# Projections with split sources: the products of a half piece in three passes, the last two half pieces by token tiles, and the norms' ends in another order

## The reference

```python
    # block 1
    merged = jax.nn.sigmoid(ga) * (ret @ w_ret_o[l]) + jax.nn.sigmoid(gb) * (att @ w_att_o[l])
    x = x + gt_a[:, None, :] * (merged @ w_o[l])
    h = modulate(rms_norm(x, g_ffn[l]), sh_f, sc_f)
...
    # block 3
    x = x + g1 * (y @ w_out[l])
    h = _rmsnorm(x, norm_ffn[l]) * (1.0 + sc2) + sh2
    u = _causal_dwconv(h @ w_up[l], conv_w[l], conv_b[l])
    u_gate, u_val = jnp.split(u, 2, axis=-1)
    x = x + g2 * ((jax.nn.silu(u_gate) * u_val) @ w_down[l])
    return _rmsnorm(x, norm_final)
```

## Time and profile before

| | us |
|---|---|
| median of 3 runs | 3537.41 |
| lowest, highest | 3537.24, 3542.29 |
| the profiled execution | 3540.02 |
| its span | 3538.3 |
| TensorE busy | 3362.9 (95% of the span), 19988 matmuls |
| DVE, ACT, POOL busy | 2047.3, 1769.5, 1046.0 |
| mean granted clock of TensorE | 0.978 |

### The profile page before, as it was taken

How to read it: one execution, slowest core, us unless ns; L and a number is a source line. 1 busy time by engine, 2 the same in 40 slices (tenths; PEclk the granted TensorE clock), 3 DMA queues, 4 the chain that set the end, 5 groups by cost and what they waited for, 6 DMA issues and landing times. The chain is left out here.

```text
span 3538.3 us, 53413 instructions
## 1 busy us (share of the span) xinstructions
PE 3362.9 (95%) x19988; PEld 2685.3 (76%) x19988; DVE 2047.3 (58%) x2355; ACT 1769.5 (50%) x2330; POOL 1046.0 (30%) x432
## 2 busy tenths in 40 slices
PE   7999999989999999999999898999999997799997
PEld 4778777768888888888888673778887766678876
DVE  3320121279999999999999725511153165346665
ACT  3322333258887878788888634432243342233333
POOL 1334222313223232323222140144443410034443
PEclk9999999989999999999999999999999988999999
DMA  8223443359999999999999737223222310022221
GB/s 278 96 72 101 125 125 125 116 205 383 378 381 370 385 367 389 367 385 375 375 378 378 264 111 264 73 94 95 96 89 79 98 40 4 7 72 95 96 95 42
DMA packets 247405, 696.18 MB, mean 197 GB/s; under 512 B 20030, under 2 KB 151858, under 8 KB 188644
## 3 DMA queue, kind: packets, MB, share of 16 engines
q1 hardware_dynamic: 237364, 658.52, 50.0%
q0 software_dynamic: 9792, 35.66, 3.8%
q10 hardware_dynamic: 112, 0.03, 0.0%
HBM read 668.90 MB, written 29.71 MB: 197 GB/s over the span
## 5 line engine op out<-in xcount | busy, mean ns | idle before, releaser
L350 POOL TENSOR_TENSOR split_w<-ring,split_w 128x1024 fp32r<-128x1024 f32 (+1 forms) x294 | 703.1, 2392 | 1569.4 <-ACT split_w L345 1492.5
L2284 DVE TENSOR_TENSOR moe_low<-ring,moe_high 128x2048 fp32r<-128x2048 f32 x408 | 929.2, 2284 | 56.8 <-ACT moe_high L2274 51.8
L2274 ACT ACTIVATE moe_high<-ring 128x1024 fp32r<-128x1024 f32 x810 | 833.4, 1063 | 123.5 <-PE psum L2525 121.4
L345 ACT ACTIVATE split_w<-ring 128x1024 fp32r<-128x1024 f32 (+1 forms) x294 | 304.3, 1036 | 970.5 <-PE psum L550 593.8
L2521 PE MATMUL psum<-moe_high,moe_xe 128*128 128x512 f32 x2176 | 585.3, 391 | 0.0
L2521 PEld LDWEIGHTS psum<-moe_high,moe_xe 128*128 128x128 f32 x2176 | 409.5, 188 | 82.4
L2433 POOL DMA_INDIRECT moe_y_rows<-moe_ye,moe_target x33 | 193.4, 5862 | 663.4 <-DVE moe_ye L2340 663.4
L550 PE MATMUL psum<-pair,split_w 128*128 128x512 f32 x1488 | 338.2, 389 | 0.0
L2525 PE MATMUL psum<-moe_low,moe_xe 128*128 128x512 f32 x1088 | 336.6, 391 | 0.1
L550 PEld LDWEIGHTS psum<-pair,split_w 128*128 128x128 f32 x1488 | 279.1, 188 | 59.7 <-issue 1.7
L550 PE MATMUL psum<-b_pair,split_w 128*128 128x512 f32 x1344 | 309.5, 391 | 0.0
(11 more groups left out here) (641 smaller groups left out, 4233.9 us busy)
## 6 DMA issues: line engine op xcount, KB each, us to landing
ring<-in_w_experts SPq DMA_DIRECT2D x408, 1024.0 KB, 8.6
ring<-in_w_mod SPq DMA_DIRECT2D x48, 1024.0 KB, 6.5
ring<-in_w_in SPq DMA_DIRECT2D x72, 512.0 KB, 5.1
ring<-in_w_up SPq DMA_DIRECT2D x33, 1024.0 KB, 5.1
ring<-in_w_in SPq DMA_DIRECT2D x25, 1024.0 KB, 5.5
ring<-in_w_down SPq DMA_DIRECT2D x20, 1024.0 KB, 5.1
ring<-in_w_gate SPq DMA_DIRECT2D x11, 1024.0 KB, 5.3
ring<-in_w_out SPq DMA_DIRECT2D x8, 1024.0 KB, 5.3
```

What stands on the lines that cost most here:

```text
L345: self.nc.scalar.activation(high, raw, ACT.Copy).then_inc(self.K.rounded, 1)
L350: self.nc.gpsimd.tensor_tensor(low, raw, high.bitcast(F32), ALU.subtract).then_inc(self.K.split, 1)
L2274: self.nc.scalar.activation(self.B["high"][:, j % HALVES, :], self.raw(j), ACT.Copy).then_inc(self.high, 1)
L2284: self.nc.vector.tensor_tensor(flat(self.low_of(j, 2)), self.K.ring[:, self.ring_slot(j // 2), :], high, ALU.subtract).then_inc(self.low, 2)
```

## The change

Six things change. (1) A half piece of kind N is multiplied in three passes over the tiles: high by high, which waits for the two rounded parts alone; low source by high weights, which waits for `a_split`; high by low weights, which waits for `split`. The last half piece of unit 0 stays in one pass where tiles are counted. (2) The last two half pieces of unit 1 are done together by `last_pieces`, tiles 0 to 2 of the one, then of the other, then tile 3 of both, so that tile 0 is complete after 24 of the last 48 matmuls, tile 1 after 30, tile 2 after 36, tile 3 after 48. (3) `DOWN_ROWS` puts the chunk of two rows second in each unit of a down projection instead of last. (4) `high_ahead` stands behind the norm's ACT steps. ACT scales tile 0 alone, and its order is square 0, root 0, square 1, root 1, square 2, scale 0, square 3, roots 2 and 3. (5) The final norm's DVE steps stand between the additions of the tiles. (6) In b2_rest the square root comes after both halves of the last chunk are rounded.

```diff
+DOWN_ROWS = ((0, 4), (4, 2), *((k, 4) for k in range(6, FFN_T, 4)))
...
-            if j == units and i == 0 and eng is nc.scalar:
+            if j == units and i == 0 and eng is nc.scalar and not tiles:
                 W.high_ahead(nc.scalar)
...
                     after.act_tiles(eng)
+                    W.high_ahead(eng)
...
+        def last_pieces(pe, out):
+
+            at = units * per - 2
+            for piece, t in ((0, 0), (0, 1), (0, 2), (1, 0), (1, 1), (1, 2), (0, 3), (1, 3)):
+                i = at + piece
+                n, place = order[i]
+                r, nr = rows_of[n, place]
+                w = W.ready(pe, n, place)
+                pe.wait_ge(a_split, min(i, per - 1) + 1 if held else i + 1)
+                x = part_of(i)[:, :, 0:nr, :]
+                for k in range(nr):
+                    for a, b in ((0, 0), (1, 0), (0, 1)):
+                        ins = nc.tensor.matmul(out[:, t, :], x[:, a, k, t * P:(t + 1) * P], w[:, b, k, :], start=False,
+                                               stop=(r + k == total - 1 and b == 1))
+                if t == NT - 1:
+                    W.used(ins, place)
+                elif piece:
+                    ins.then_inc(tiles, 1)
...
+                    by_tile = tiles and i == (j + 1) * per - 1
+                    for parts_now in ([((0, 0), (1, 0), (0, 1))] if by_tile else [((0, 0),), ((1, 0),), ((0, 1),)]):
+                        w = W.ready_high(pe, n, place)
+                        if not paired:
+                            pe.wait_ge(a_high, source_no)
+                        if (0, 1) in parts_now:
+                            W.ready(pe, n, place)
+                        if (1, 0) in parts_now and not paired:
+                            pe.wait_ge(a_split, source_no)
+                        for t in range(NT):
+                            for k in range(nr):
+                                for a, b in parts_now:
...
-        self.scaled_by_act = (0, 1) if gated else ()
+        self.scaled_by_act = (0,) if gated else ()
...
-        square(0)
-        for t in range(NT):
-            if t < NT - 1:
-                square(t + 1)
+        for t in range(2):
+            square(t)
             root(t)
-            if t in (1, 2):
-                scale(t - 1)
+        square(2)
+        scale(0)
+        square(3)
+        for t in (2, 3):
+            root(t)
...
+    def dve_tile(self, ve, t):
+
+        if t:
+            self.dve_var(ve, t - 1)
+        if t > 1:
+            ve.wait_ge(self.loaded, 16)
+            self.dve_out(ve, t - 2)
+        if t == NT - 1:
+            self.dve_var(ve, t)
+            self.dve_out(ve, 2)
+            self.dve_out(ve, 3)
...
                     if j == 2:
                         evacuate(0)
+                    if j == 3:
                         sc.wait_ge(var, 1)
```

53 lines of the change are left out of this document (24 added, 29 removed).

## The result

| | before | after |
|---|---|---|
| median, us | 3537.41 (3536.60 to 3547.16, 5 runs) | 3518.59 (3511.24 to 3521.33, 5 runs) |
| the profiled execution | 3540.02 | 3516.78 |
| its span | 3538.3 | 3514.9 |
| TensorE busy | 3362.9 | 3357.8 |
| mean granted clock | 0.978 | 0.982 |

The ratio of the runs is 0.9935, 95% interval 0.9924 to 0.9946: 23 us faster (19 to 27). The two medians alone differ by 18.8. The forecast was 3524.4, 13.0 faster. The sign was right, the size was not.

What follows compares the result with a forecast made beforehand. TensorE is busy 95% of the span, so gains lie where it stands still or work follows its last matmul. Terms 2.2 + 1.0 + 2.1 + 3.9 + 3.8 = 13.0 from the median 3537.4 gave 3524.4, range 3518 to 3531.

Steps and rivals of the forecast that it cites:

- (1) b2_rest: In b2_rest, with the root behind both roundings, TensorE's wait of 2.21 us goes: gain 2.2, between 0 and 2.2.
- (2) b2_down: In b2_down's products, 2.8 us lost before and 1.8 to 1.9 after: gain 1.0, between 2.0 and -0.5.
- (3) b3_down: In b3_down's products, 9.1 us lost before and 6.9 after: gain 2.1, between 5 and -1.5.
- the 1.6 that I put down to 1.2 GHz: At the unit's end in b3_down before: 1.6 us counted as lost because TensorE ran at 1.2 GHz from 3460.3 to 3463.6.
- (4) the end: At the program's end, last tile written 7.1 us after the last matmul instead of 11.0: gain 3.9 (3.0 to 4.5).
- (5) the tails: Norms behind w_o, b3_out, b2_down and b2_out: gains of 0.7, 1.2, 1.5 and 0.4 us, together 3.8.
- I take 7.4: Behind w_o and b3_out, first evacuation 7.4 us after the last matmul, at 1.2 GHz, instead of 5.6 at 2.4 GHz.
- more clock freed: Rival: two or three stretches at 1.2 GHz in the tails vanish, giving 3519.5; chance 0.11 (3516 to 3521).
- (6): high_ahead behind the norm's last root on ACT costs nothing while ACT's wait covers it; the pass boundaries also cost 0.
- The boundaries: 134 added pass boundaries in 67 half pieces cost 0; the rival had 0.188 us each, 3549.6, chance 0.04 (above 3540).
- the first rival: POOL's split starts before DVE's last scaling in three norms, 1.2 us a stage: 3528; chance 0.13, shared with stops kept.

Runs made afterwards that it cites:

- s3_ends_alone: The kernel before with only the norm's order, the final norm's DVE steps and the root of b2_rest changed; 3537.76 us, ratio 0.9982 to before.
- s4_no_rows: The changed kernel with the chunk of two rows last in each unit again; 3523.42 us, ratio 0.9945 to before.
- s8_before_fill: The kernel before with transposes of the identity in TensorE's gaps in the tails behind w_o and b3_out; one trace, 3536.99 us.
- s2_passes_alone: The kernel before with half pieces in three passes and their waits, everything else as before; 3525.75 us, ratio 0.9949 to before.

## Why the prediction was right in sign and wrong in size

- **(1) b2_rest**, 2.2: -2.49. The whole wait is gone. In half of before's traces a stretch at 1.2 GHz went with it, 1.5 more.
- **(2) b2_down**, 1.0: -0.6. Stops of 0.58 twice where 0.5 stood, 0.95 in the last 48 where 0.9 stood.
- **(3) b3_down**, lost 6.9: 7.1 by the same count. Head 3.0 (3.4 forecast), unit 1's head 2.15 (2.5), last pieces 0.95 (0.9), each at its place; the rest are mostly the restarts behind them. What it gains by that is less sure: before lost 9.1 in the trace that I read, 11.9 and 12.3 in two others, so that 2.1 against -2.25 is a hit for that trace only. And the 1.6 that I put down to 1.2 GHz cost nothing by itself: without it the third stop was 2.76.
- **(4) the end**, 7.1 behind the last matmul: 6.7. DVE's order alone gives 0.95 of the 4.29 (`s3_ends_alone`); the rest needs the tiles that come earlier, 2.65 of it the order of rows (`s4_no_rows`).
- **(5) the tails**: here is the step that failed. The 3.8 came out as 8.8. The chain of steps was right (first evacuation forecast at 5.6 and 4.9 for 2.4 GHz, measured at 5.5 and 4.8); the clock was wrong. "It has as little to do after, so I take 7.4" did not count how long TensorE stands: 3.2 in two pieces before, 2.1 in three after (b3_out). With both prices written down I took the slow one three times; `s8_before_fill` shows the 1.7 and 2.2 that the clock alone makes in `w_o` and `b3_out`. For `b2_down`, the third, no run had its tail with the change and at 1.2 GHz, so that its share is argued. The rival "more clock freed" (3519.5) was the case that came, and had 0.11.
- **(6)** `high_ahead` costs nothing behind the norm: right, and ahead of it it would have cost 16. The boundaries cost nothing: right, shown by `s2_passes_alone`. POOL started 0.3 behind DVE's last scaling, the margin that the first rival rested on, and it was 0.29 in all three tails of the changed kernel's trace.
- **A term that was missing.** The sum had 0 for code that the change does not touch. There the profile pair shows -5.0, and the ratio's 23 less the stages' 18.4 about as much; a pure delay shows that such a sum can be 9 off without any work gained. Which of untouched code's stretches at 1.2 GHz vanish, and why, stays open. The range, 3518 to 3531, was made of the terms' bounds alone, and of a clock that costs 1.6 a piece; before's own executions (3534.52 to 3553.52) differ by more than its width.
